# Four instead of three block-saving steps of eight in each tile pair of the first feed-forward

## The reference

```python
hn = rmsnorm(h, ffn_norm[l])
h = h + (jax.nn.silu(hn @ w_gate[l]) * (hn @ w_up[l])) @ w_down[l]
```

## Time and profile before

| | |
|---|---|
| time, median of 3 runs | 2432.6 us (2431.69 to 2432.75) |
| span of the profiled execution, first to last instruction | 2429.9 us |
| PE busy | 2417.6 us (99%) |
| DVE busy | 1881.4 us (77%) |
| ACT busy | 1387.7 us (57%) |
| granted TensorE clock, mean | 0.999 |
| f1 to f10 in the span | about 643.8 to 1067.9 us |

### The profile page before, as it was taken

One profiled execution on the slowest core, in us unless ns is written; L12 is line 12 of the kernel. 1 busy time (PEld: TensorE's weight loads), 2 busy tenths in 40 slices (PEclk: granted clock), 3 DMA queues, 4 the chain that ended last, 5 costly groups with the idle time before them and its releaser, 6 DMA issues.

```text
span 2429.9 us, 29002 instructions
## 1 busy us (share of the span) xinstructions
PE 2417.6 (99%) x11145; PEld 2008.2 (83%) x11145; DVE 1881.4 (77%) x2411; ACT 1387.7 (57%) x1744; POOL 50.6 (2%) x93
## 2 busy tenths in 40 slices
PE   9999999999999999999999999999999999999998
PEld 7888888888888888888888888888788888888887
DVE  6455555688898888989777587664889999999877
ACT  6446555445655555556456464564666666666554
POOL 1000110000000000000001100000000000000000
PEclk9999999999999999999999999999999999999999
DMA  7655555666666666666666555566566666666675
GB/s 238 198 172 155 185 156 162 217 192 191 191 197 200 201 195 203 195 192 202 197 208 198 167 154 161 155 191 197 167 197 193 196 200 188 194 195 189 200 215 169
DMA packets 239299, 460.11 MB, mean 189 GB/s; under 512 B 16582, under 2 KB 18800, under 8 KB 238528
## 3 DMA queue, kind: packets, MB, share of 16 engines
q1 hardware_dynamic: 237760, 452.65, 61.2%
q0 software_dynamic: 1376, 5.69, 0.7%
q10 hardware_dynamic: 32, 0.01, 0.0%
HBM read 456.19 MB, written 2.10 MB: 189 GB/s over the span
## 4 chain that ended last, share of the span: by engine, by line
PE 98%; DVE 1%; DMA 0%; SPq 0%; issue 0%; ACT 0%; DVEq 0%; ACTq 0%
PE acc L1005 16%; PE acc L1007 16%; PE acc L1006 16%; PE acc L721 11%; PE acc L723 11%; PE acc L722 11%; PE mis L1006 3%; PE mis L1005 3%; PE mis L1007 3%; PE mis L694 1%; PE mis L1290 1%; PE mis L819 1%; PE mis L1199 1%; PE acc L740 1%; PE acc L741 1%; PE acc L742 1%
## 5 line engine op out<-in xcount | busy, mean ns | idle before, releaser
L1601 ACT ACTIVATE wf<-wf_raw 128x1024 fp32r<-128x1024 f32 x544 | 568.4, 1058 | 548.3 <-DVE wf_raw L2431 219.1
L2443 DVE TENSOR_TENSOR wf<-wf_raw,wf 128x1024 fp32r<-128x1024 f32 x544 | 643.3, 1219 | 79.1 <-ACT wf L1601 75.6
L2099 DVE TENSOR_TENSOR lo<-raw,hi 128x1024 fp32r<-128x1024 f32 (+1 forms) x313 | 376.5, 1219 | 231.1 <-ACT hi L1354 228.7
L1354 ACT ACTIVATE hi<-raw 128x1024 fp32r<-128x1024 f32 (+1 forms) x313 | 321.0, 1049 | 162.9 <-PE acc L723 139.0
L1005 PE MATMUL acc<-wf,xb_hi 128*128 128x512 f32 x931 | 365.3, 392 | 0.0
L1007 PE MATMUL acc<-wf,xb_lo 128*128 128x512 f32 x931 | 362.7, 390 | 0.0
L1006 PE MATMUL acc<-wf,xb_hi 128*128 128x512 f32 x931 | 362.3, 389 | 0.0
L721 PE MATMUL acc<-hi,xa_hi 128*128 128x512 f32 (+1 forms) x576 | 224.4, 390 | 0.0
L723 PE MATMUL acc<-hi,xa_lo 128*128 128x512 f32 (+1 forms) x576 | 221.8, 385 | 0.0
L722 PE MATMUL acc<-lo,xa_hi 128*128 128x512 f32 (+1 forms) x576 | 221.6, 385 | 0.0
L721 PE MATMUL acc<-hi,xb_hi 128*128 128x512 f32 x544 | 216.4, 398 | 0.0
(11 more groups left out here) (530 smaller groups left out, 3800.0 us busy)
## 6 DMA issues: line engine op xcount, KB each, us to landing
raw<-in_w_in SPq DMA_DIRECT2D x215, 512.0 KB, 4.2
wf_raw<-in_w_ffn_in SPq DMA_DIRECT2D x160, 512.0 KB, 3.7
wf_raw<-in_w_gate SPq DMA_DIRECT2D x88, 512.0 KB, 3.7
wf_raw<-in_w_up SPq DMA_DIRECT2D x88, 512.0 KB, 3.8
wf_raw<-in_w_down SPq DMA_DIRECT2D x88, 512.0 KB, 4.5
wf_raw<-in_w_ffn_out SPq DMA_DIRECT2D x88, 512.0 KB, 4.0
wf_raw<-in_w_out SPq DMA_DIRECT2D x32, 512.0 KB, 4.5
raw<-in_w_o SPq DMA_DIRECT2D x32, 512.0 KB, 4.9
```

The source lines that it names most:

```text
L1354: nc.scalar.activation(hi[:, slot, :, 0:width], raw[:, slot, :, 0:width], ACT.Copy)\
L1601: nc.scalar.activation(wf[:, f_slot[c], 0, :, :], wf_raw[:, f_slot[c], 1, :, :], ACT.Copy)\
L2099: V.tensor_tensor(lo[:, slot, :, 0:width], raw[:, slot, :, 0:width], hi[:, slot, :, 0:width].bitcast(F32), ALU.subtract).then_inc(lo_ready, 1)
L2443: V.tensor_tensor(wf[:, f_slot[c], 1, :, :], wf_raw[:, f_slot[c], 1, :, :], wf[:, f_slot[c], 0, :, :].bitcast(F32), ALU.subtract).then_inc ...
```

## The change

In f1 to f10 the k pairs 0, 2, 4 and 5 are seven-product ones, where 0, 3 and 5 were. In f0 a fourth set of activation forms is made; it is placed in `xo`, a buffer that the projection `out` used before. In the loop over the pairs `gated_up` stands behind the work for k = 2, and ACT's `t_hi_of` calls move with their k pairs. The stages `out` and `ffn2` keep their (0, 3, 5).

```diff
-F_S = (0, 3, 5)
+S_K = dict(out=(0, 3, 5), ffn=(0, 2, 4, 5), ffn2=(0, 3, 5))
+S_AT = dict(out=(3, 1, 2), ffn=(0, 3, 1, 2), ffn2=(0, 1, 2))
...
         def x_place(stage, q):
 
-            return (xo[:, 0], xo_raw[:, 0]) if stage == "out" and q == 0 else (xf[:, q], xf_raw[:, q])
+            j = S_AT[stage][q]
+            return (xo[:, 0], xo_raw[:, 0]) if j == 3 else (xf[:, j], xf_raw[:, j])
...
             f_hi_of(f0, 7, 0)
+            x_form_hi("ffn", 3)
             f_hi_of(f0, 7, 1)
...
                 f_hi_of(p, 2, 1)
                 f_hi_of(p, 3, 0)
+                t_hi_of(p, 2)
                 f_hi_of(p, 3, 1)
                 f_hi_of(p, 4, 0)
-                t_hi_of(p, 3)
                 f_hi_of(p, 4, 1)
                 f_hi_of(p, 5, 0)
+                t_hi_of(p, 4)
                 f_hi_of(p, 5, 1)
                 f_hi_of(p, 6, 0)
                 t_hi_of(p, 5)
...
             x_form_lo("ffn", 2)
+            x_forms("ffn", 3)
             f_lo_of(f0, 7, 0)
             f_lo_of(f0, 7, 1)
+            x_form_lo("ffn", 3)
...
             for p in ffn_b:
                 f_lo_of(p, 1, 1)
-                f_lo_of(p, 2, 0)
+                strassen(p, 2)
                 gated_up(run_b[p.no - 1])
-                f_lo_of(p, 2, 1)
-                strassen(p, 3)
-                f_lo_of(p, 4, 0)
-                f_lo_of(p, 4, 1)
+                f_lo_of(p, 3, 0)
+                f_lo_of(p, 3, 1)
+                strassen(p, 4)
                 strassen(p, 5)
```

More of the change, by code:

```diff
@@ L107 @@
 O_S = (3, 5)
-X_ORDERS = ((0, 1, 2), (0, 1, 2), (0, 1, 2))
 E_S = ()
@@ L499, in two_blocks @@
                 for i in range(first, dict(out=DT // 2, ffn=FT, ffn2=FT, down=DT // 2, down2=DT // 2)[stage]):
-                    nk, forms = KD // CK, F_S
+                    nk, forms = KD // CK, S_K.get(stage)
                     if stage in ("down", "down2"):
@@ L503, in two_blocks @@
                     elif i == first:
-                        forms = dict(out=O_S, ffn=E_S, ffn2=F_S[1:])[stage]
+                        forms = dict(out=O_S, ffn=E_S, ffn2=S_K["ffn2"][1:])[stage]
                     p = Pair(sum(map(len, runs)), run, stage, i, nk, forms, c, g, tile0)
@@ L536, in forms_due @@
         def forms_due(stage, q):
-            at = ("out", "ffn", "ffn2").index(stage)
-            return len(F_S) * at + X_ORDERS[at].index(q) + 1
+            before = ("out", "ffn", "ffn2").index(stage)
+            return sum(len(S_K[s]) for s in ("out", "ffn", "ffn2")[:before]) + q + 1
         def x_place(stage, q):
-            return (xo[:, 0], xo_raw[:, 0]) if stage == "out" and q == 0 else (xf[:, q], xf_raw[:, q])
+            j = S_AT[stage][q]
+            return (xo[:, 0], xo_raw[:, 0]) if j == 3 else (xf[:, j], xf_raw[:, j])
         def sums_of(p):
@@ L1047, in forms @@
                 if p.wide:
-                    return [[x_place(p.stage, F_S.index(k))[0][:, j, f, :] for j in range(2)] for f in range(4)]
+                    return [[x_place(p.stage, S_K[p.stage].index(k))[0][:, j, f, :] for j in range(2)] for f in range(4)]
                 if p.run:
@@ L1072, in strassen @@
                 if p.wide and p.i <= p.run + 1:
-                    pe.wait_ge(xf_lo, forms_due(p.stage, F_S.index(k)))
+                    pe.wait_ge(xf_lo, forms_due(p.stage, S_K[p.stage].index(k)))
                 if p is e1 and k in E_AGAIN:
@@ L2395, in x_forms @@
             def x_forms(stage, q):
-                k, x, n = F_S[q], xa if stage == "out" else xb, forms_due(stage, q)
+                k, x, n = S_K[stage][q], xa if stage == "out" else xb, forms_due(stage, q)
                 if n > 1:
```

## The result

The changed kernel takes 2441.68 us (median of 5, 2440.75 to 2443.02) against 2432.6 for the kernel before: ratio 1.0038, 95% interval 1.0026 to 1.0051. It is slower, by 9.1 us where 7.8 were forecast (2440.4), inside the range. The profiled span grew by more, from 2429.9 to 2440.0 us: in every run here with both on record, time and span are 1.7 to 1.9 us apart and not 2.7, so the profiled execution of the kernel before was a fast one, of about 2431.7 us (the first of its three runs, 2431.69). About 0.9 us of the 10.1 is that.

A forecast was written before the change was run, and what follows sets the result against it. PE bounded the kernel before; after the change, a loop through PE, SP's load, ACT and DVE would pace. 5.5 + 2.5 - 0.2 = 7.8 us made the span 2437.7; with 2.7 around it, 2440.4 us, range 2434 to 2446.

The forecast's parts named there:

- What PE saves: In each pair of f1 to f10, one product of three matmuls fewer: 0.68 us, an unhindered period of 41.71.
- What DVE must do more: In each pair, sums and a t difference add 4.34 us, making DVE's work 42.1 us.
- Where DVE waits, and the chain behind it: DVE waits at k = 2 until 9.76 us, then works 26.85 to `y_ok`; each pair 0.69 us longer.
- The ends: Outside f2 to f9: +2.5 us for f0 and f1 from the fourth set of forms, -0.2 for f10.
- the hand-over from `y_ok` to the turn: At the end of each pair, from DVE's `y_ok` to PE's `turn`: 0.12 us.
- f10: Last pair: no next sums ahead of `middle_end`, `y_ok` at 35.4, PE there at 35.9; -0.2 us.
- DVE's load alone: Rival for the pairs: chunk (3,0) comes early enough, DVE's work paces at 42.1 us; 2432.0 us, chance 0.17.
- PE paces: Rival for the pairs: DVE's added work under 3.9 us and all waits gone; 2428.2 us, chance 0.04.
- a price of PE's stops beyond their length: Rival: PE's waits also lower its clock, 13 us more, 2453; smaller form, slower hand-over, +1.5; chance 0.09.

The follow-up runs named there:

- e12: The changed kernel with e9's edits, DVE's gated product left out, and seven-product k pairs 0, 2, 3, 5 in place of 0, 2, 4, 5: 2426.79 us.
- e1: The changed kernel with ACT's t copy of k = 2 moved ahead of its hi copy of chunk (3,0): 2434.71 us.
- e9: e1 with the third and fourth sets of activation forms made earlier in f0: 2431.25 us.
- e5: The changed kernel with one unused DVE instruction of 1.14 us per pair in f1 to f10, ahead of DVE's work for k = 2: 2444.03 us.
- e6: The changed kernel with one unused DVE instruction of 1.14 us per pair in f1 to f10, behind the gated product: 2454.36 us.
- e10: e1 with DVE's gated product left out and done by nobody, for timing only: 2434.27 us.
- e7: e1 with the gated product made by GpSimd instead of DVE: 2452.44 us.

## Why the prediction was right, step by step

- **What PE saves** (0.68 us per pair): right. e12's period of 41.80 is 0.59 under 42.39, and PE still waits there a little; PE's own was put at 41.71.
- **What DVE must do more** (4.34 us, 42.1 per pair in all): right within 0.2; e1 and e9 put the work at 41.9 to 42.0 (period less DVE's waits).
- **Where DVE waits, and the chain behind it**: right to 0.04 us in the place of each step up to `y_ok`, and shown by e1 (take it away), e5 and e6 (load each side of it). Period 43.08, as forecast; f2 to f9 cost 5.6 where 5.5 were forecast. That the period fits to the last digit is luck: the loads took 0.04 more on average and the way from the turn to the next pair 0.05 more (6.40 for 6.35), while the hand-over from `y_ok` to the turn took 0.05 for 0.12, and the chain 0.03 less.
- **The ends**: right in kind, short in size. f0 and f1 were put at 2.5 and came to 4.33 in the trace. Of this 0.7 is not the change's: the transposes ahead of f0's first forms stand 0.73 later already (592.00 against 591.27 us), as the starts of that place differ by up to 1.35 us among the profiled runs. Another 0.5 is a wait of DVE for ACT ahead of `f_lo(7,1)` in f0, which the sum did not have, and 0.4 a wait for a chunk at k = 4 of f1, where I had written that no data wait lies inside the chain. The term was undersized by about 1.1 us.
- **f10**: put at -0.2, came to +0.2. `y_ok` did come early, as forecast, and PE does not wait for it; but (3,0) came 0.2 late there, so the t difference started at 9.96, and PE, stopped longer at k = 5, reached the turn at 36.20 instead of 35.9.
- **The rivals**: "DVE's load alone" is what e1 makes of the kernel, not what the change is; its price of 2432.0 was 2.7 us short of e1, whose pairs took 42.36 for the 42.1 put there and whose forms cost more than 2.4. "PE paces" asked for DVE's added work under 3.9 us and for all waits to be gone: e10 met the first and not the second, by a loop that I had not seen. The granted clock stayed at 1.00 through f1 to f10, in the changed kernel and in e6, whose stops on PE are longer. What e6 cost beyond its instructions is in the landing of its loads; there is no sign of a price of PE's stops beyond their length.

What stays open: whether a layout with all outputs kept can reach PE's 41.71. It would need 0.2 to 0.3 us less of DVE's work per pair from somewhere other than GpSimd; k pairs 0, 2, 3, 5 with the gated product in place were not run.

## What to carry to other kernels

Removing work from the bounding engine pays only if the partner that feeds it has time for what it gets in exchange: compare the partner's work, not its busy share, with the new period, before anything else. Then follow, from each point where a queue waits for something that the bounding engine itself released (here a ring slot), the chain back to the next thing it waits for: each such loop has a period of its own, and removing the slowest shows the next (43.08, 42.2, 41.8 here). An idle engine is no free place for an instruction if its work stretches that of the busy one, as GpSimd's did here.

## What was not expected of the hardware

GpSimd's elementwise work beside DVE's two-input instructions: 1.3 to 4.1 us for 128x512 on GpSimd (in f2 to f9 of e7, on average 2.3 for the scaled copy and 1.7 for the product), and a DVE instruction of 0.68 us stretched to 1.78. Four GpSimd instructions, which replaced 1.3 us of DVE's queue, cost DVE 2.6.
